# The 32 sample tokens of token-stationary units as plain 4-byte matmuls in four column tiles, taken from raw weights

## What is computed

```python
xn = rms_norm(x, norm_g)
h = einsum('btd,de->bte', xn, w_in)
qa, ka, va, ua, qi, ki, wi, qb, kb, vb, ub, ga, gb = split(h)   # 512 columns each; ki 64, wi 8, ga and gb 1024
qa, ka = rope(rms_norm(qa)), rope(rms_norm(ka)); qi = rope(qi); ki = rope(rms_norm(ki))
A = softmax attention over the topk keys by  sum_h relu(qi . ki) * wi
B = stick-breaking attention (no softmax), strictly causal, of qb, kb, vb
y = x + w_o( sigmoid(ga) * W_A[A * silu(ua)] + sigmoid(gb) * W_B[B * silu(ub)] )
```

## Time and profile before

| | us |
|---|---|
| median of 3 runs | 523.32 (523.22 to 523.72) |
| profiled execution, its time | 523.65 |
| profiled execution, span from first to last instruction | 521.9 |
| PE busy | 515.1 (99%) |
| DVE busy | 370.7 (71%) |
| ACT busy | 258.2 (49%) |
| POOL busy | 76.7 (15%) |

### The profile page before, as it was taken

The page is one execution under the profiler, slowest core; times in us unless marked ns, Lnnn a source line. Parts: engine busy times, 40 slices in busy tenths (PEclk is TensorE's granted clock), DMA queues, the critical chain, the costliest instruction groups (busy, mean ns, idle before and its releaser), DMA issues.

```text
span 521.9 us, 10124 instructions
## 1 busy us (share of the span) xinstructions
PE 515.1 (99%) x4188; PEld 485.5 (93%) x4188; DVE 370.7 (71%) x718; ACT 258.2 (49%) x434; POOL 76.7 (15%) x73
## 2 busy tenths in 40 slices
PE   8999999999999999999999999999999999999997
PEld 6889999999998988989998888999999999999997
DVE  5878758899979989478857668563987556665331
ACT  7655764344366566864244665653566532231100
POOL 3506000014034314284000000000000000000000
PEclk9999999999999999999999999999999999999999
DMA  7623305142331322023230016020232172245111
GB/s 274 266 80 123 92 1 167 35 168 82 117 133 28 140 82 82 1 82 122 87 113 4 1 47 212 2 82 1 82 105 98 42 252 80 82 162 189 50 52 46
DMA packets 15359, 50.45 MB, mean 97 GB/s; under 512 B 2288, under 2 KB 6000, under 8 KB 11728
## 3 DMA queue, kind: packets, MB, share of 16 engines
q1 hardware_dynamic: 15168, 49.49, 27.6%
q10 hardware_dynamic: 144, 0.30, 0.2%
HBM read 42.82 MB, written 6.82 MB: 95 GB/s over the span
## 4 chain that ended last, share of the span: by engine, by line
PE 91%; DVE 4%; issue 2%; ACT 2%; DMA 1%; ACTq 0%
PE PS L665 40%; PE PS L1004 9%; PE PS L958 8%; PE PS L989 8%; PE PS L619 4%; PE PS L784 3%; PE PS L765 3%; PE PS L649 3%; PE PS L869 2%; PE PS L741 2%; PE PS L710 2%; PE PS L849 1%; PE PS L690 1%; PE PS L598 1%; PE PS L793 1%
## 5 line engine op out<-in xcount | busy, mean ns | idle before, releaser
L665 PE MATMUL PS<-xhi,whi 128*128 128x272 f32 x320 | 94.6, 296 | 0.0
L665 PE MATMUL PS<-xlo,whi 128*128 128x272 f32 x320 | 92.4, 289 | 0.0
L665 PE MATMUL PS<-xhi,wlo 128*128 128x272 f32 x320 | 92.1, 288 | 0.0
L1452 DVE TENSOR_TENSOR wlo<-raw,whi 128x2048 fp32r<-128x2048 f32 (+1 forms) x31 | 64.5, 2080 | 17.3 <-ACT whi L1051 15.9
L665 PE MATMUL PS<-whi,xhi 128*128 128x256 f32 x256 | 73.4, 287 | 0.8 <-DVE nmx L1844 0.8
L665 PE MATMUL PS<-wlo,xhi 128*128 128x256 f32 x256 | 72.4, 283 | 0.0
L665 PE MATMUL PS<-whi,xlo 128*128 128x256 f32 x256 | 71.9, 281 | 0.0
L665 PEld LDWEIGHTS PS<-xhi,whi 128*128 128x128 f32 x320 | 60.3, 189 | 2.9 <-issue 2.3
L1051 ACT ACTIVATE whi<-raw 128x2048 fp32r<-128x2048 f32 (+1 forms) x31 | 52.1, 1682 | 18.2 <-PE PS L1004 18.2
L665 PEld LDWEIGHTS PS<-xhi,wlo 128*128 128x128 f32 x320 | 60.4, 189 | 0.0
L665 PEld LDWEIGHTS PS<-xlo,whi 128*128 128x128 f32 x320 | 60.2, 188 | 0.0
(11 more groups left out here) (283 smaller groups left out, 1318.2 us busy)
## 6 DMA issues: line engine op xcount, KB each, us to landing
raw<-in_w_units SPq DMA_DIRECT2D x28, 1024.0 KB, 4.9
raw<-in_w_mixes SPq DMA_DIRECT2D x8, 512.0 KB, 3.4
stage<-in_x_kw_qi SPq DMA_DIRECT2D x7, 564.5 KB, 5.1
res<-in_x_kw_qi SPq DMA_DIRECT2D x1, 2176.0 KB, 8.1
out<-res SPq DMA_DIRECT2D x16, 136.0 KB, 1.7
out<-vals SPq DMA_DIRECT2D x2, 1024.0 KB, 6.2
out<-kT SPq DMA_DIRECT2D x1, 1088.0 KB, 8.7
out<-tm SPq DMA_DIRECT2D x1, 1024.0 KB, 8.0
```

The costliest lines, as they stand in the source:

```text
L665: mm = pe.matmul(out, lhsT, rhs, start=(k == 0), stop=(k == 23))
L1452: dve.tensor_tensor(wlo[:, uu % 2, 0:n], raw[:, uu % 2, 0:n], whi[:, uu % 2, 0:n].bitcast(F32), ALU.subtract).then_inc(w_lo, 1)
```

## The change

For the eight token-stationary units the sample's 16 fp32r matmuls become 32 plain 4-byte matmuls. `xst` now holds the 32 rows as 4-byte numbers (POOL adds high and low part). The 256 weight columns are cut in four pieces of 64, and piece q goes to the column tile q of the array: stationary operand 128x32, output in partitions 32q to 32q+31 of the bank. The moving operand is the raw block itself. ACT copies the four pieces out in four instructions; the addition on POOL and its semaphore `sample_rows` are gone. The same is done for qi (four pieces of 128 columns per chunk, from the staged raw weights `first_of(c)`).

As the sample group now needs only the raw block, it is the first of its unit's five groups, except in vb0, where it stays last. And as PE now reads `raw`, `load_unit` of unit u also waits for the sample group of unit u-2.

```diff
-        GROUPS += [(_u, t) for t in range(5)]
+        GROUPS += [(_u, t) for t in ((4, 0, 1, 2, 3) if _u else range(5))]
...
+def sample_group(u):
+    return FIRST_GROUP[u] + (4 if u == 0 else 0)
...
                 elif uu >= 2:
                     sp.wait_ge(w_lo, direct_index(uu - 2) + 1)
+                    if UNITS[uu - 2][1] == "tm":
+                        sp.wait_ge(group_done, sample_group(uu - 2) + 1)
...
+            def samples(c):
+                for q in range(4):
+                    mm = pe.matmul(ps[DEC * q:DEC * q + DEC, 4, 0:P], xst[:, c, :],
+                                   first_of(c)[:, KW + P * q:KW + P * q + P], start=(c == 0), stop=(c == KC - 1),
+                                   skip_group_check=True)
...
-                for b in range(2):
-                    mm = pe.matmul(ps[0:2 * DEC, 4, :], xst[:, c, :], fpart[b][:, c, KW:FIRST],
-                                   start=False, stop=(c == KC - 1 and b == 1))
-                mm.then_inc(chunk_done if c < KC - 1 else qi_done, 1)
+                samples(c).then_inc(chunk_done if c < KC - 1 else qi_done, 1)
...
-                if g == FIRST_GROUP[uu]:
+                if UNITS[uu][1] == "tm" and part == 4:
+                    pe.wait_ge(raw_ready[uu % 2], raw_count(uu))
+                elif g == (tile_group(UNITS[uu][0], 0) if UNITS[uu][1] == "tm" and uu else FIRST_GROUP[uu]):
                     pe.wait_ge(w_lo, direct_index(uu) + 1)
...
                     for c in range(KC):
-                        for b in range(2):
-                            mm = pe.matmul(bank[0:2 * DEC, 0:UC], xst[:, c, :], wview(wpart[b], uu)[:, c, :],
-                                           start=(c + b == 0), stop=(c + b == KC))
+                        for q in range(4):
+                            w = by(KC, raw[:, uu % 2, :])[:, c, UC // 4 * q:UC // 4 * (q + 1)]
+                            mm = pe.matmul(bank[DEC * q:DEC * q + DEC, 0:UC // 4], xst[:, c, :], w,
+                                           start=(c == 0), stop=(c == KC - 1), skip_group_check=True)
...
-                ins = act.activation(dst, bank[0:n, 0:UC], ACT.Copy)
                 if t == 4:
-                    k = sample_units(name)
-                    if k >= 2:
-                        act.wait_ge(sample_rows, k - 1)
-                    ins = act.activation(low_part[0:DEC, :], bank[DEC:2 * DEC, 0:UC], ACT.Copy)
+                    for q in range(4):
+                        ins = act.activation(dst[:, UC // 4 * q:UC // 4 * (q + 1)],
+                                             bank[DEC * q:DEC * q + DEC, 0:UC // 4], ACT.Copy)
+                else:
+                    ins = act.activation(dst, bank[0:n, 0:UC], ACT.Copy)
...
-                pool.tensor_copy(xst[:, c, 0:DEC], xhi[:, c, SEQ:NT].bitcast(F32))
-                pool.tensor_copy(xst[:, c, DEC:2 * DEC], xlo[:, c, SEQ:NT].bitcast(F32)).then_inc(x_st, 1)
+                pool.tensor_tensor(xst[:, c, :], xhi[:, c, SEQ:NT].bitcast(F32), xlo[:, c, SEQ:NT].bitcast(F32),
+                                   ALU.add).then_inc(x_st, 1)
```

More of the change, by code:

```diff
@@ L589, in _ @@
             pe.wait_ge(x_st, 1)
-            for b in range(2):
-                mm = pe.matmul(ps[0:2 * DEC, 4, :], xst[:, 0, :], fpart[b][:, 0, KW:FIRST], start=(b == 0), stop=False)
-            mm.then_inc(chunk_done, 1)
+            def samples(c):
[3 more added lines that the diff above has]
+                                   skip_group_check=True)
+                return mm
+            samples(0).then_inc(chunk_done, 1)
             for c in range(1, KC):
@@ L612, in _ @@
                     for tt in range(5):
[L613 removed]
+                        s0, m = (P * tt, P) if tt < 4 else (SEQ, 4 * DEC)
                         ss = pe.matmul(ps[0:m, 5, 2 * tt:2 * tt + 2], x_sum[:, s0:s0 + m], unity,
@@ L807, in _ @@
                         pe.wait_ge(cache_bv_in, 16)
-                        pe.wait_ge(sample_rows, sample_units("vb1"))
                         group_out_wait(pe, LAST_GROUP[U["vb1"]])
@@ L883, in weigh_a @@
                     pe.wait_ge(cache_av_in, 16)
-                    pe.wait_ge(sample_rows, sample_units("va1"))
+                    group_out_wait(pe, LAST_GROUP[U["va1"]])
                 if t >= 3 and t % 3 == 0:
@@ L1111, in _ @@
                 if t == 4:
-                    act.activation(qi_low, ps[DEC:2 * DEC, 4, :], ACT.Copy, scale=xrs[DEC:2 * DEC, 4:5])
+                    for q in range(4):
+                        v = slice(DEC * q, DEC * q + DEC)
+                        last = act.activation(tm[0:DEC, 4, P * q:P * q + P], ps[v, 4, 0:P], ACT.Copy, scale=xrs[v, 4:5])
+                    last.then_inc(qi_out, 1)
+                    break
                 act.activation(tm[0:n, t, 0:W], ps[0:n, t, :], ACT.Copy, scale=xrs[0:n, t:t + 1]).then_inc(qi_out, 1)
@@ L1312, in high_b @@
                     act.wait_ge(s3_low, 1)
-                    act.wait_ge(sample_rows, sample_units("va1"))
                 act.wait_ge(pv_out, 5)
@@ L2050, in _ @@
             pool.wait_ge(qi_out, 5)
-            pool.tensor_tensor(tm[0:DEC, 4, 0:W], tm[0:DEC, 4, 0:W], qi_low, ALU.add).then_inc(qi_rows, 1)
             link(pool.tensor_copy(ident_b, ident))
@@ L2061, in _ @@
             pool.affine_select(later, later, [[1, P]], ALU.is_ge, 0.0, base=0, channel_multiplier=-1).then_inc(const_ready, 1)
-            def add_sample(name):
-                group_out_wait(pool, LAST_GROUP[U[name]])
-                c = UC * int(name[2])
-                if name[0] == "v":
-                    dst = vals[0:DEC, 6, c:c + UC]
-                else:
-                    c += W if name[:2] == "ka" else 0
-                    dst = tm[0:DEC, 4, c:c + UC]
-                pool.tensor_tensor(dst, dst, low_part[0:DEC, :], ALU.add).then_inc(sample_rows, 1)
-            add_sample("vb0")
             def weights(t):
@@ L2094, in roots @@
                 pool.tensor_tensor(nrs[0:n, t, :], nss[0:n, t, :], halves[0:n, 0:H], ALU.pow).then_inc(rooted, 1)
-            for g in DOT_FILL:
-                filled(g)
-            for k, g in enumerate(PRE_B):
-                filled(g)
+            for k in range(len(PRE_B)):
                 if K_SQUARE + 2 <= k < K_SQUARE + 7:
```

45 lines of the change are left out of this document (14 added, 31 removed).

## The result

The changed kernel takes 529.31 us (median of 4, 528.36 to 530.67). Runs of the kernel before on the same chip gave 523.52 (523.22 to 523.81). The ratio is 1.0113, 95% interval 1.0087 to 1.0138, so the change makes the kernel 1.1% slower. The prediction said 529.5, slower. The profiled execution took 529.89 at a span of 528.2; it stands 6.2 us over the profiled one of before.

The account below looks back on a forecast made before the run. PE, 99% busy, bounds the kernel. Items +0.45, first wait +4.55, second +3.6, six units -3.9, va1 -0.45 give +4.25 us on 523.32, 527.6; one clock fall makes 529.5, range 524.8 to 533.5.

Parts of the forecast that it names:

- The sample group: Each unit's sample on PE: 64 passes, four column tiles side by side, 1.20 us against 1.87, 0.65 us saved per unit.
- qi: The qi matmuls, 8 chunks: 0.54 us per chunk instead of 0.46, adding 0.65 us and delaying all that follows.
- The items: Transposed items after vb0's sample: DVE's rows come 0.65 us later, so items start 0.45 us later, at 53.95.
- First wait: PE before vb1's tile 1: ka0's raw block loads late, ACT runs 4.3 us later, PE waits 4.4 us; +4.55 with pacing.
- Second wait: PE in the dots after ka0's tile 0: indexer key stores queue behind kb0's load, 3.15 us idle; 3.6 with slower dots.
- Moves that cost nothing: Later fetches, two more small ACT copies per unit, POOL's additions gone: no PE wait; attention A loses 0.2 us of gain.
- The clock: PE's clock falls at least in the first wait; about 4 us at half speed lose 2 us: 529.5 us, chance 0.45.
- seven units after vb0: Sample groups of vb1, ka0, ka1, qa0, qa1, va0 save 3.9 us together, and va1 saves 0.45.
- no wait, 519.4: Rival: no wait reaches PE, its own saving stands alone, 519.4 us; chance 0.08.
- the two that price the passes: Rivals: passes limited by issue, 532.7 us, chance 0.09; column tiles don't overlap, 548 us, chance 0.04.
- Two waits, clock never falls: Rival: both waits occur on PE but the clock stays at full, 527.6 us; chance 0.27.
- only one wait: Rival: the stores land at once, so only one wait reaches PE, 525.0 us with the clock at full; chance 0.07.

Follow-up runs that it names:

- experiments 7 to 9: Experiment 6 with the eight units' sample groups in one column tile (7: 539.06 us), two in turn (8: 524.92), or four run tile by tile (9: 534.60).
- experiment 10: Experiment 6 plus one 32x480 addition on POOL beside DVE's rows, its result unused: 520.19 us.
- experiment 2: Changed kernel with ka0's high part on ACT and low part on DVE moved behind the transposed items: 523.62 us.
- experiment 5: Changed kernel with vb0's sample group alone reading the split halves in 128 passes, so ka0's raw block loads early: 524.84 us.
- experiment 1: Changed kernel with SP issuing the two stores of the indexer's keys before kb0's load: 525.93 us.
- experiment 6: Experiment 3 plus ACT's turned copy in attention B put before the next unit's high part: 518.68 us.
- experiment 3: Changed kernel with the moves of experiment 1 and experiment 2 together: 519.63 us.
- experiment 4: Changed kernel with 60 extra unused matmuls on PE, 38 before vb1's tile 0 and 22 before ka0's: 527.75 us.

## Why the prediction was right

The two waits, what causes them and the fall of the clock are those that the runs show, and 529.5 stands 0.2 from the measured 529.31. That it is so close is luck in two ways. Several terms were off and made up for each other: the items, the second wait and the units came out 2.0 us lower than their terms, the clock and a third wait 1.7 us higher. And the text gave 529.5 for one fall of the clock and 531.3 for two, where the executions with one took 528.4 and 528.7 and those with two 529.9 and 530.7: like for like it was 1 us too high, and the median lies between the two kinds.

- **The sample group**: 0.65 us saved at vb0, as sized; in all eight groups the 64 passes take 0.88 us from their first start to their last. What the text had to choose, full overlap of four tiles at one 64-column pass per 0.056 us, is the mechanism (experiments 7 to 9).
- **qi** was mis-sized. A chunk is 0.05 to 0.06 us longer instead of 0.08 (35.42 to 31.43 was 3.99 us between the sample's starts, 35.63 to 31.58 is 4.05), and between 21.3 and 27.0 us the changed kernel gets back about 0.2, so that q i ends 0.15 us late and not 0.65.
- **The items** came 0.55 early, not 0.45 late, 1.0 us of the sum. The step that failed is "they come 0.65 later": DVE's rows end at 52.67, 0.6 before, since the five scalings take 1.05 us less without POOL's addition beside them (experiment 10 brings 0.76 of that back with a somewhat smaller addition). So the items start as soon as PE is free. The text said of POOL's additions that nobody waited for them on PE. True, but DVE shared their time.
- **First wait**: 4.66 us, predicted 4.4, and for the reason given: ka0's high part starts at 57.96 (predicted 58.65). Its end came 0.6 early (64.50 instead of 65.1), since vb0's sample had ended early. Experiment 2 removes it, and experiment 5 leaves 0.72 us of it.
- **Second wait**: 2.55 us where 3.15 was predicted, from the stores (predicted at 79.4 and 79.85, issued at 79.97 and 80.44). ACT goes on at 85.37, 0.67 later than predicted, but PE came to its dot at 84.13. The text said 82.95, a slip of 0.3: its own terms (79.0, 1.4 and 2.85) make 83.25. Of the 0.9 us beyond that, 0.4 were there at the end of ka0's sample, since the first wait ended 0.6 early but the fall behind it, which this step left out, took 1.6, and the groups between were 0.6 shorter than charged; and 0.47 came in the four dots behind the sample. Experiment 1 removes the wait.
- **"Moves that cost nothing"** failed twice. qa0 and qa1's groups have another order now: a long tile stands where the short sample group was, and ACT's copy for attention B falls behind a high part of 1.9 us. 0.44 us of idle time, 0.6 us in the end (experiment 6). The text named a third wait as what would prove it wrong; it was there, and small. And the four dots behind ka0's sample take 1.87 us instead of 1.41, in experiment 3 too (73.47 to 75.34). The short sample stands ahead of them now in place of a long tile, and PE gets there while ACT, which made a high part first, is still at the relus from 78.71 on, 0.48 us apart. Experiments 7 to 9 bear that out: behind their longer sample groups the same four dots take 1.50 to 1.51 us.
- **The clock** fell, as forecast, for 1.6 us per fall instead of 2. The prediction counted one fall; the profiled execution had two, at both waits, and half of the executions had one. Which of the two was missing there isn't recorded: the first wait alone brought a fall in all four executions of experiment 1, the second alone in all ten of experiment 2, and with the second wait whole experiment 5 had one in five of ten. The 2 us for a fall came from some 4 us at half speed at PE's start; the low stretches inside the kernel last 3.4. The reading that PE began at the half level stands, as these rows of PE in the kernel before show:

```profile
5.01 1.05 PE L587 MATMUL PS<-fhi,xhi 128*128 128x512 f32 x2
5.86 0.39 PE L583 MATMUL PS<-xhi,fhi 128*72 128x272 f32 x1
...
6.68 0.62 PE L587 MATMUL PS<-fhi,xlo 128*128 128x512 f32 x2
7.14 0.29 PE L583 MATMUL PS<-xlo,fhi 128*72 128x272 f32 x1
```

| us | predicted | traces, after against before |
|---|---|---|
| to the start of the items | +0.45 | -0.55 |
| first wait with its pacing | +4.55 | +4.66 |
| second wait with its pacing | +3.6 | +2.55 and some 0.4 |
| third wait | 0 | +0.6 |
| clock | +2.0 | +3.1 (the profiled one fell twice; 0.2 coincides with the slow dots) |
| seven units after vb0 | -4.35 | -4.7 |
| sum | +6.25 | +6.1 |

PE's last matmul ends 6.1 us later than before, and the time of the profiled execution is 6.2 longer. The row of the units is experiment 3 against the kernel before, from the start of the items to PE's end: 465.8 us before, 461.7 there, of which the third wait is 0.6. It isn't seven times 0.65. From the items to attention B three units gave only 1.7 us (88.0 us, then 86.3), since they include the slow dots; in attention B three gave 2.4, 0.8 each (141.6 us, then 139.8 with the third wait in it). The whole comes out near eight times 0.65 less 0.15 for q i, 5.05: experiment 6, with all three waits gone, is 5.16 under the kernel before. The rival "no wait, 519.4" is thus the kernel of experiments 3 and 6, at 519.63 and 518.68.

Of the rivals, the two that price the passes are refuted. Issue takes 6 to 7 ns between tiles, not 22. The Trainium skill's floor of 25 ns from start to start (TensorE: Matmul & The Clock Gate, Wait — 56ns, not 53.3ns?) doesn't hold for passes in different column tiles; the trace shows 14 ns in the mean (0.88 us over 63 starts), and by that rule the time would have been 5 us longer. "Two waits, clock never falls" is refuted by the stretches at 0.50 and by experiment 4, "only one wait" by the timeline of PE (its 525.0 should have been 524.0, 527.6 less 3.6).

## What to carry to other kernels

A cheaper instruction can be the smallest part of its change: here the matmuls gave 5.2 us, and what they read (`raw` in place of its copies) held back DMA issues at two places, which cost 9.7 us of PE. When an operand is read from another buffer, list who waits for that buffer to be free and then everything queued behind those waits on their engines, as one moved load and two moved stores were almost the whole loss and three moved lines gave it back. Small matmuls in different column tiles should go round the tiles, not tile by tile, and be followed by a look at the clock wherever PE has come to idle.

## What the runs showed of the hardware

- Plain 4-byte passes of 64 columns: 56 ns each in one column tile, and four tiles at once at the same 56 ns, starts 6 to 7 ns apart.
- Passes of different tiles also mix when they aren't next to each other: tile by tile, 2.96 us instead of 3.54.
- In the profiled executions the granted clock fell to 0.50 around both idle times of 4.6 us (changed kernel, experiment 1) and around all three of 2.5 us (changed kernel, experiments 2 and 5), and not in experiment 4 with 1.4 us. By the mean clocks, experiment 5 had no fall in five of its ten executions. It isn't a matter of length alone: in the execution of experiment 6 that took 520.83, PE idled 0.77 us up to 22.84 and then worked from 25.1 to 28.5 at 0.50, as the rows below show, while idle times of 0.79 and 1.09 us late in the kernel (up to 303.25 and 476.86 us in the changed one) were followed by no fall in any profiled execution. Each stretch at 0.50 inside a kernel lasted 3.4 us.
- At its start PE runs at the half level: starts of 512-column matmuls stand 0.42 us apart, and 0.23 from the first record of the granted clock on, which comes at 4.6 us (experiment 6) to 7.7 us (experiment 1).
- An addition of 32x480 on POOL, 0.98 us long, makes DVE's five operations beside it 0.76 us longer. The Trainium skill (SBUF — State Buffer, Who interferes with whom) says that a DVE instruction with two inputs in SBUF contends with a GpSimd one that reads SBUF. `SCALAR_TENSOR_TENSOR tm<-tm,nrs,gk` is such a one, and the trace agrees: 0.76 us lost beside 0.98.
- Sums of several column ranges in the same partitions of one bank, begun in turn, did not come out whole (relative error of the outputs with sample rows 0.30 to 0.40 with four ranges, 0.25 to 0.32 with two), where four tiles with partitions of their own are whole. The cause wasn't tried. The Trainium skill (PSUM — Partial Sum Buffer, The four PSUM rules) says that the first matmul of a sum clears the marks of what was written in the whole bank for its 32 partitions, so that the next product of another sum begun there overwrites instead of adding. No run here shows those marks.

The stretches of that execution of experiment 6:

```profile
22.00:22.80 0.80, 0.07 (x1) 0.00 (x0) 0.77 (x3) 0.80 (x1) 0.00 (x0) 1.00 1.03 425
22.80:24.80 2.00, 1.96 (x14) 1.82 (x15) 1.52 (x3) 1.11 (x1) 0.92 (x2) 1.00 0.29 109
...
25.20:28.00 2.80, 2.80 (x8) 2.05 (x7) 1.94 (x1) 0.83 (x2) 0.82 (x1) 0.50 0.00 0
```
